# Attention with keys on the partitions, and a state scan made in four stretches

## What is computed

```python
def one_block(qblk):
    s = jnp.einsum('bgrqd,bgkd->bgrqk', qblk, kt).astype(jnp.float32) * scale
    p = jax.nn.softmax(s, axis=-1).astype(vt.dtype)
    return jnp.einsum('bgrqk,bgkd->bgrqd', p, vt)

def s5_bidirectional(u, ...):
    for direction, reverse in ((0, False), (1, True)):
        a_bar = jnp.exp(a * dt)                       # one complex number a state
        bu = jnp.einsum('blgp,gnp->blgn', ug, b_bar)
        _, states = lax.associative_scan(_linear_combine, (a_seq, bu), axis=1, reverse=reverse)
        y = y + jnp.einsum('blgn,gpn->blgp', states, c).real
```

## Time and profile before

| | us |
|---|---|
| median of 3 runs | 2836.97 |
| lowest, highest | 2826.1, 2838.0 |
| profiled execution, own time | 2827.34 |
| span of its trace | 2825.2 |
| the stage `heads` with its barriers, 547 to 904 | 357 |
| the stage `s5_outputs`, 904 to 1040 | 136 |

### The profile page before, as it was taken

One profiled execution on the slowest core, in us unless ns is written; L12 is line 12 of the kernel. 1 busy time (PEld: TensorE's weight loads), 2 busy tenths in 40 slices (PEclk: granted clock), 3 DMA queues, 4 the chain that ended last, 5 costly groups with the idle time before them and its releaser, 6 DMA issues. The chain is left out here.

```text
span 2825.2 us, 41292 instructions
## 1 busy us (share of the span) xinstructions
PE 2560.4 (91%) x15638; PEld 2207.0 (78%) x15638; DVE 1403.6 (50%) x2285; ACT 923.0 (33%) x1916; POOL 1134.5 (40%) x1244
## 2 busy tenths in 40 slices
PE   6999997699997868799799999999999699999798
PEld 6988886699996657677678888877777589998587
DVE  6464444687887936322654453555555522222314
ACT  4232222633333233223322223356565400000321
POOL 3454441177775125402054544433333355552320
PEclk9999999999998889899999999999999799999899
DMA  7323333201011464444343333343432464442543
GB/s 162 113 65 106 102 106 89 56 24 47 31 39 31 74 128 153 133 158 144 115 103 129 117 144 125 132 164 125 148 121 104 175 202 136 136 136 83 195 148 149
DMA packets 268360, 328.33 MB, mean 116 GB/s; under 512 B 45300, under 2 KB 216974, under 8 KB 267030
## 3 DMA queue, kind: packets, MB, share of 16 engines
q1 hardware_dynamic: 230006, 239.09, 28.3%
q10 hardware_dynamic: 38176, 86.78, 8.3%
HBM read 212.75 MB, written 103.55 MB: 112 GB/s over the span
## 5 line engine op out<-in xcount | busy, mean ns | idle before, releaser
L1025 POOL TENSOR_TENSOR w_hi<-w_raw,ones 128x512 fp32r<-128x512 f32 (+1 forms) x232 | 274.8, 1184 | 765.4 <-PE r L1036 263.8
L1027 POOL TENSOR_TENSOR w_lo<-w_raw,w_hi 128x512 fp32r<-128x512 f32 (+1 forms) x232 | 344.8, 1486 | 18.2
L1036 PE MATMUL r<-h_lo,w_hi 128*128 128x264 f32 (+1 forms) x864 | 286.6, 332 | 0.0
L1036 PE MATMUL r<-h_hi,w_lo 128*128 128x264 f32 (+1 forms) x864 | 278.5, 322 | 0.0
L1036 PE MATMUL r<-h_hi,w_hi 128*128 128x264 f32 (+1 forms) x864 | 277.6, 321 | 0.0
L1036 PE MATMUL r<-xc_lo,w_hi 128*128 128x264 f32 (+1 forms) x768 | 248.5, 324 | 28.4 <-POOL w_lo L1027 28.4
L1036 PE MATMUL r<-xc_hi,w_lo 128*128 128x264 f32 (+1 forms) x768 | 248.9, 324 | 0.0
L1036 PE MATMUL r<-xc_hi,w_hi 128*128 128x264 f32 (+1 forms) x768 | 248.4, 323 | 0.0
L434 POOL TENSOR_TENSOR w_lo<-w_raw,w_hi 128x512 fp32r<-128x512 f32 x64 | 85.2, 1359 | 251.0 <-ACT w_hi L500 251.0
L1036 PEld LDWEIGHTS r<-xc_lo,w_hi 128*128 128x128 f32 x768 | 146.0, 190 | 41.0 <-issue 28.9
L1036 PEld LDWEIGHTS r<-h_hi,w_hi 128*128 128x128 f32 x864 | 163.0, 189 | 16.2 <-issue 2.4
(11 more groups left out here) (345 smaller groups left out, 6376.0 us busy)
## 6 DMA issues: line engine op xcount, KB each, us to landing
w_raw<-in_w_in_even SPq DMA_DIRECT2D x72, 256.0 KB, 3.0
w_raw<-in_w_in_odd SPq DMA_DIRECT2D x64, 256.0 KB, 3.4
w_raw<-in_w_ogate SPq DMA_DIRECT2D x64, 256.0 KB, 7.1
v_d<-vs ACTq DMA_DIRECT2D x8, 1152.0 KB, 4.2
us<-u_d SPq DMA_DIRECT2D x128, 65.0 KB, 2.9
xc_d<-xc ACTq DMA_DIRECT2D x8, 1040.0 KB, 6.4
qk_d<-qk ACTq DMA_DIRECT2D x16, 520.0 KB, 2.7
sz_d<-sz SPq DMA_DIRECT2D x8, 1040.0 KB, 5.2
```

The source lines that it names most:

```text
L1025: self.nc.gpsimd.tensor_tensor(hi, raw, one, ALU.mult).then_inc(self.hi_done, 1)
L1027: self.nc.gpsimd.tensor_tensor(lo, raw, hi.bitcast(F32), ALU.subtract).then_inc(self.split, 1)
L1036: ins = self.nc.tensor.matmul(bank[:, 0:n], w[:, u % self.buffers, k, :], z[:, off:off + n], start=(first and k == 0 and w is self.hi and ...
```

## The change

**Attention.** The keys now lie on the partitions. A head's queries are two parts of 580 and 460 (`PARTS`), so there are 16 passes; in each, the nine blocks of 116 keys (`KEYS`) are steps. In a step PE makes the scores [116 keys, 580 or 460 queries] (`scores`), ACT copies them from the PSUM into the tile `prob` (`keep`), and DVE raises a running maximum `top` with them (`higher`: both inputs in SBUF). At the end of a pass PE turns `top` around (`turn_top`), DVE finds each query's maximum (`find`), PE spreads it over the partitions (`spread`), DVE subtracts it from the stored scores (`lower`: one input in SBUF, one in PSUM), ACT takes the exponential in place (`power`), and the result is already what PE needs as weights for the product with the values (`mix`), which come with a column of ones that gives the sum of each row. The 648 transposes of probabilities fall away; there are 72 for the maxima, 72 for spreading and 72 to turn the finished [queries, 128] tiles (`turn_rows`). A finished tile is copied by ACT, its sum inverted by DVE (`invert`), scaled by ACT, turned by PE and multiplied with the gate by DVE (`out`). The order of all this is written out by hand again: pass n's scores, pass n-1's subtraction and pass n-2's product with the values run in the same nine steps.

**Scan.** The 130 chunks, with two of zeros behind them, are four stretches of 33. POOL first scans the four side by side (32 steps: one product of 1024 columns and two additions of 512), then carries the ends of the stretches on (two steps with `far`, the 33rd power of `step`), and then adds to each chunk of the last three stretches what comes from the stretch before (32 steps: one product of 768 columns, two additions of 384). Every instruction waits for the one before it. It is written out, without a loop. `far` is made in `front` by 36 small DVE instructions and four copies. POOL's scratch is `pw_in`, which is not needed any more then; `s5_outputs` uses the same room.

The diff, cut to its core; the removed lines of `heads` and `s5_scan` are in the listing above.

```diff
-QT = [(0, 120), (120, 120), (240, 112), (352, 120), (472, 112), (584, 112),
-      (696, 120), (816, 112), (928, 112)]
+KEYS = [(i * 116, min(116, L - i * 116)) for i in range(NT)]
+PARTS = [(0, 580, 5, 116), (580, 460, 4, 115)]
+START = (222, 0)
...
-            vt = se.sb("v", [P, NT, KV * HD])
+            vt = se.sb("v", [P, NT, KV, HD + 1])
...
-            t["Z"] = se.sb("Z", [P, CH + 1, 2, G])
+            t["Z"] = se.sb("Z", [P, 1 + SUPER * LONG, 2, G])
...
+SUPER, LONG = 4, 33
 def s5_scan(nc, gp, t, tmp, steps, turns):
     do = Steps(gp, steps)
     tt = nc.gpsimd.tensor_tensor
+    z = t["Z"][:, 1:1 + SUPER * LONG, :, :].rearrange("p (s j) q g -> p s j (q g)", s=SUPER)
+    carry = tmp[1]
+    def product(now, factor):
+        n = now.shape[1]
+        out = tmp[0][:, 0:n * 4 * G].rearrange("p (s o q) -> p s o q", s=n, o=2)
+        do(tt(out, now.unsqueeze(2).broadcast_to([P, n, 2, 2 * G]),
+              t[factor][:, :, :].rearrange("p (o q) g -> p o (q g)", o=2).unsqueeze(1).broadcast_to([P, n, 2, 2 * G]),
+              ALU.mult))
+        return out[:, :, :, 0:G], out[:, :, :, G:2 * G]
+    def add(out, x, y):
+        do(tt(out, x, y, ALU.add))
+    def halves(x):
+        return x.rearrange("p s (o g) -> p s o g", o=2)
+    for j in range(1, LONG):
+        own, other = product(z[:, :, j - 1, :], "step")
+        now = halves(z[:, :, j, :])
+        add(now, now, own)
+        add(now, now, other)
+    for s in range(1, SUPER - 1):
+        own, other = product(z[:, s - 1:s, LONG - 1, :], "far")
+        now = halves(z[:, s:s + 1, LONG - 1, :])
+        add(now, now, own)
+        add(now, now, other)
+    left = z[:, 0:SUPER - 1, LONG - 1, :]
+    for j in range(LONG - 1):
+        own, other = product(left, "step")
+        add(carry[:, :, :, :], own, other)
+        left = carry[:, :, :, :].rearrange("p s o g -> p s (o g)")
+        now = halves(z[:, 1:SUPER, j, :])
+        add(now, now, carry[:, :, :, :])
...
-        tmp = s.sb("tmp", [P, 2, GB // 2, T, GP])
+        tmp = t["pw_in"][:, :, :, :].rearrange("p e q g -> p (e q g)").rearrange(
...
+                one, power = (pw[:, T, 0, :], pw[:, T, 1, :]), (X(0), X(1))
+                times(power, one, one)
+                for n in range((LONG - 1).bit_length() - 2):
+                    times(power, power, power)
+                times(power, power, one)
+                do.free(v.tensor_copy(t["far"][:, 0, :], X(0)))
...
+    LOWERED = {0: ((2, 8),), 3: ((1, 0),), 4: ((1, 1), (1, 2)), 5: ((1, 3),), 6: ((1, 4), (1, 5)), 7: ((1, 6),),
+               8: ((1, 7),)}
...
+        sb = s.sb("prob", [P, NB, NT, WIDE])
+        top, peak = s.sb("top", [P, WIDE]), s.sb("peak", [P, 5])
...
+                def scores(n, j):
+                    off, width, tiles, m = PARTS[n % 2]
+                    ko, kn = KEYS[j]
+                    g = n // 2 % KV
+                    if j == 0:
+                        pe.wait_ge(q_done, n + 1)
+                        if n >= 2:
+                            pe.wait_ge(found, n - 1)
+                        if n and turned_in[n - 1]:
+                            pe.wait_ge(yd, turned_in[n - 1])
+                    elif j == 1:
+                        if n >= 2:
+                            pe.wait_ge(low, NT * (n - 1))
+                    else:
+                        pe.wait_ge(kept, NT * n + j - 1)
+                    out = region(n, j)
+                    for o, w in HALVES[n % 2]:
                         for x, z in ((0, 1), (0, 0), (1, 0)):
+                            last = nc.tensor.matmul(out[0:kn, START[n % 2] + o:START[n % 2] + o + w],
+                                                    kr[z][:, g, ko:ko + kn], q[x][:, off + o:off + o + w],
+                                                    start=(z == 1), stop=(x == 1))
+                    last.then_inc(sc, 1)
...
+                def turn_top(n):
+                    off, width, tiles, m = PARTS[n % 2]
+                    pe.wait_ge(kept, NT * n + 8)
...
+                def mix(n, j):
+                    off, width, tiles, m = PARTS[n % 2]
+                    g = n // 2 % KV
+                    for x in range(j * tiles, (j + 1) * tiles):
+                        i, k = divmod(x, NT)
+                        w = DONE[n] + i
+                        if i == 0:
+                            pe.wait_ge(ex, NT * n + k + 1)
+                        if k == 0 and w >= 2:
+                            pe.wait_ge(taken, w - 1)
+                        kn = KEYS[k][1]
+                        last = nc.tensor.matmul(o_slot(w)[0:m, :], sb[0:kn, n % NB, k, i * m:(i + 1) * m],
+                                                vt[0:kn, k, g, :], start=(k == 0), stop=(k == NT - 1))
+                        if k == NT - 1:
+                            last.then_inc(pv, 1)
...
+                for n in range(LAST + 1):
+                    for j in range(NT):
+                        if n < NU:
+                            scores(n, j)
+                        if j == 2 and 1 <= n <= NU:
+                            spread(n - 1)
+                        if 2 <= n < LAST:
+                            mix(n - 2, j)
+                        for w in turned_at.get(n * NT + j, ()):
+                            turn_rows(w, n)
+                        if j == 0 and 1 <= n <= NU:
+                            turn_top(n - 1)
...
+                def keep(n, j):
+                    kn, width = KEYS[j][1], PARTS[n % 2][1]
+                    if j == 0 and n >= NB:
+                        act.wait_ge(pv, DONE[n - NB + 1])
+                    act.wait_ge(sc, NT * n + j + 1)
+                    nc.scalar.activation(sb[0:kn, n % NB, j, 0:width],
+                                         region(n, j)[0:kn, START[n % 2]:START[n % 2] + width],
+                                         ACT.Copy).then_inc(kept, 1)
+                def power(n, j):
+                    kn, width = KEYS[j][1], PARTS[n % 2][1]
+                    act.wait_ge(low, NT * n + j + 1)
+                    nc.scalar.activation(sb[0:kn, n % NB, j, 0:width], sb[0:kn, n % NB, j, 0:width], ACT.Exp,
+                                         scale=SCALE).then_inc(ex, 1)
...
+                for n in range(LAST + 1):
+                    for j in range(NT):
+                        for w in mixed_at.get(n * NT + j - 1, ()):
+                            take_rows(w)
+                        if n < NU:
+                            keep(n, j)
+                        for back, k in LOWERED.get(j, ()):
+                            if 0 <= n - back < NU:
+                                power(n - back, k)
+                        for w in mixed_at.get(n * NT + j - 1, ()):
+                            scale_rows(w)
+                        if j == 4 and n + 1 < NU:
+                            leading(n + 1)
...
+                def higher(n, j):
+                    kn, width = KEYS[j][1], PARTS[n % 2][1]
+                    dve.wait_ge(kept, NT * n + j + 1)
+                    now = sb[0:kn, n % NB, j, 0:width]
+                    if j == 1:
+                        if n:
+                            dve.wait_ge(tt, n)
+                        v.tensor_tensor(top[0:kn, 0:width], sb[0:kn, n % NB, 0, 0:width], now,
+                                        ALU.max).then_inc(raised, 1)
+                    else:
+                        dve.wait_ge(raised, (NT - 1) * n + j - 1)
+                        v.tensor_tensor(top[0:kn, 0:width], top[0:kn, 0:width], now, ALU.max).then_inc(raised, 1)
...
+                def lower(n, j):
+                    kn, width = KEYS[j][1], PARTS[n % 2][1]
+                    if j == 0:
+                        dve.wait_ge(sp_done, n + 1)
+                    dve.wait_ge(kept, NT * n + j + 1)
+                    x = sb[0:kn, n % NB, j, 0:width]
+                    at = SPREAD_AT[n % 2]
+                    v.tensor_tensor(x, x, region(n, NT + 1)[0:kn, at:at + width], ALU.subtract).then_inc(low, 1)
...
+                for n in range(LAST + 1):
+                    for j in range(NT):
+                        if j == 1 and 1 <= n <= NU:
+                            find(n - 1)
+                        for w in mixed_at.get(n * NT + j - 1, ()):
+                            invert(w)
+                        for w in out_at.get(n * NT + j, ()):
+                            out(w, n)
+                        for back, k in LOWERED.get(j, ()):
+                            if 0 <= n - back < NU:
+                                lower(n - back, k)
+                        if n < NU and j:
+                            higher(n, j)
+                        if j == 5 and n + 1 < NU:
+                            rest(n + 1)
```

More of the change, by code:

```diff
@@ new lines, in spread @@
+                def spread(n):
+                    off, width, tiles, m = PARTS[n % 2]
+                    pe.wait_ge(found, n + 1)
+                    pe.wait_ge(kept, NT * (n + 1))
+                    out = region(n, NT + 1)
```

(26 more changed lines are left out.)

296 lines of the change are left out of this document (133 added, 163 removed).

## The result

The changed kernel takes **2866.5 us** (median of 4 runs, 2865.5 to 2867.9) beside 2834.6 us for the kernel before (4 runs, 2826.1 to 2838.0): ratio **1.0117, 95% interval 1.0093 to 1.0142**. It is slower by 32 us. The forecast was 2833, and the likeliest case was no change, with a range of its own of 2819 to 2851; the measured time lies outside that, and at the upper edge of the wide range (2793 to 2868). Times near 2873 stood in the text as the third case, at 0.19.

What follows compares the result with a forecast made beforehand. PE was taken to bound attention now, with POOL's scan 8 us ahead; after the change, scan and attention would end near 898 and 893, saving 4 us: 2837 - 4 = 2833 us on the median's footing, range 2793 to 2868.

Steps and rivals of the forecast that it cites:

- the likeliest case: In `heads`, POOL's scan slowed by `higher` sets the end, attention close; stage within 14 us of now; chance 0.43.
- The third case: In attention, DVE becomes the bound, each `higher` waiting 0.97 us; stage 36 us later, whole 2873 us; chance 0.19.
- What a wait costs: In attention, DVE's `higher` and `rest` wait for POOL 0.65 us on average, 144 times, 94 us in all.
- `lower` pays nothing: In attention, DVE's `lower` reads PSUM and is free of sharing with POOL, staying near 0.76 us.
- POOL: The new scan takes 303 us alone, ending at 850; sharing with DVE adds 48 us, so it ends at 898.
- PE: In attention, PE's work falls from 342 to 301 us; were PE the bound, attention would end at 865.
- The step that failed: In attention, waits raise DVE from 243 to 337 us, passing PE's 301; attention ends near 893.
- DVE's own sum: DVE's instructions in attention take 30.4 us a head, 243 us in all, less than PE's 301.
- The skill's rule: DVE instructions with two SBUF inputs contend with POOL reading SBUF; the second blocks fully, for the whole instruction.
- 100 us of it for POOL: In the scan, POOL loses each `higher`'s whole length, 100 us; stage 47 us later, 2884 us; chance 0.06.
- the 48 that came from the rows of `ogate`: In the scan, each `higher` costs POOL 0.40 us at 580 columns, 0.27 at 460: 48 us.
- The 40 small instructions in `front`: On DVE in `front`, 8 to 10 us, hidden ahead of an 18.00 us idle gap, so nothing behind it moves.

Runs made afterwards that it cites:

- Experiment 1: The changed kernel with the state scan on POOL left out beside attention: 2785.9 us, ratio 0.9838 to the kernel before.
- experiment 12: The changed kernel without its scan, DVE filling 335 columns with zeros before each of 144 `higher` and `rest`: 2812.6 us, ratio 0.9932.
- Experiment 3: The kernel before with only the new scan, its attention as before: 2863.8 us, ratio 1.0114.
- experiment 2: The changed kernel with the running maximum reading the new scores from PSUM, PE waiting before it overwrites them: 2801.8 us, ratio 0.9892.
- the doses: Two runs of the changed kernel without its scan, DVE zero fills before 144 instructions: 745 columns, 2857.9 us; 335 columns, 2812.6 us.
- experiment 7: The changed kernel with the running maximum read from PSUM and the state scan left out: 2793.9 us, ratio 0.9867.
- experiment 4: The changed kernel with the scan of the kernel before: 2837.8 us, ratio 1.002.
- Experiment 5: The changed kernel with each product of the new scan made in two instructions of half the width: 2843.7 us, ratio 1.0036.
- experiment 9: The changed kernel with a finished row turned by PE one step later: 2863.3 us, ratio 1.0112.
- experiment 11: The changed kernel without its scan, DVE filling 745 columns with zeros before each of 144 `higher` and `rest`: 2857.9 us, ratio 1.0093.

## Why the prediction was wrong

Step by step, by its own numbers.

- **What a wait costs: right in all, with some luck.** 0.65 us on average for each of 144, 94 us in all, was the forecast; 0.68 and 98 were measured, and `higher` at 1.58 us for the "near 1.4" that was named. Beside the wide steps (to 741) a wait is 0.86 us where 0.75 was worked out, beside the adding steps 0.55 for 0.54, and the last 8 of the 144 come when POOL is done and wait for nothing, which the forecast had not taken off. It was also right that `lower` pays nothing.
- **POOL: right.** The scan was to end at 898, and at 850 if alone. It ends at 894.8; with the PSUM read, where POOL shares with 16 instructions only, at 851.5.
- **PE: nearly right.** 301 us were forecast, and attention's end at 865 with PE alone. Experiment 1 has 281 us, and 857.9: 20 us less work, and 13 us more idle time than the 17 that the forecast allowed up to attention's end, so the near hit is in part two errors against each other. The 302 us of the kernel after look like a hit and are none: they are experiment 1's 281 and 21 more for the same 2160 records at a lower clock (0.93 for 0.98).
- **The step that failed: what DVE's waits were added to.** The prediction added 94 us to DVE's own 243, got an end of 893, and compared it with PE's 865 and POOL's 898, as if three queues ran side by side and the longest decided. By that, DVE had 58 us of slack to give. DVE's own sum was not the fault: without POOL the window shows it busy 216 us, with the overlap of neighbours counted once, and the forecast's 243 is the sum of lengths. But the order of a pass closes a loop. PE's scores go to ACT's copy, DVE's maximum, PE's turn and spread, DVE's subtraction, ACT's exponential and back to PE, in a hand-written order with each engine's queue in it. A sum that fits the runs starts from PE's path and adds most of the waits to it: attention alone ends at 858, the waits add 98, and with shares of 0.66 to 0.86 that gives 923 to 942; 935.5 was measured (a share of 0.79). The share comes from the experiments and was not to be had from the profile before; with a share of 1 the same working would have said 956.
- **The third case** named this ("a late `higher` holds `turn_top`, ACT and then PE") and gave 2873, close to what came. That its time came out near is partly luck: it still compared the sums of queues, with a mean wait of 0.97 us that was not met, and held that it decides only from 0.80 on (its own sum passes POOL's 898 at 0.69). Attention set the end at 0.68, and in experiment 12 an addition of 0.23 us a piece (33 us over 144) already moves the end of attention by 23 us.
- **The skill's rule.** `higher`, with two inputs in SBUF, waits beside POOL, and `lower` does not. The Trainium skill, "SBUF — State Buffer", section Who interferes with whom, states just this of one and of two SBUF inputs; the trace agrees. For two SBUF inputs the full blocking that the prediction quotes stands in another section of that page, Summary: rules for kernel authors: the second to issue blocks until the first has finished. The prediction made 100 us of it for POOL; POOL lost 43, near the 48 that came from the rows of `ogate`, where 0.14 us of each start overlap. Experiment 3 met another sentence of Who interferes with whom, that a `tensor_scalar` can contend as well: the scaling takes 0.76 us at its shortest, 0.86 on average beside the old scan's short instructions and 1.60 beside the wide ones. The prediction had left that out.
- The 40 small instructions in `front` cost nothing that shows at the start of `heads`, 547 in both kernels. But 36 of them take 13.0 us, where 8 to 10 were forecast for all 40; the idle gap ahead of the copy of C shrinks from 18.00 to 3.49 us, and that copy starts 0.8 us later.

Where does the gain of the lighter PE go? Against the kernel before, attention without a scan gained 43 us (the old attention was not run without its scan, so this is the new one alone against the old one with it), and lost 78 to the scan that runs beside it. Of these 78, by the windows of experiment 1 and the kernel after, 57 are idle time of PE (86.6 us for 29.5) and 21 are PE's own work taking longer; by the ratio of the clocks, 0.98 to 0.93, some 15 of the 21 are the clock (an estimate). With experiment 2 most of it comes back, and that the cure is one operand of one instruction is the plainest sign that DVE's waits beside POOL are the cause.

What stays open: why the share is 0.7 in one case and 0.86 in another; by which of the waits in the loop DVE's lost time reaches PE, since the doses show only that it arrives, and the loop itself is read from the code and from one place of the timeline; and the 4 us that the kernel after loses behind the stage.

## What to carry to other kernels

When a step runs round a loop of three engines, don't just compare their sums: here 0.66 to 0.86 of the time that DVE lost was added to the stage, although DVE was idle nearly a third of the time. That it holds for the other engines of the loop was not tried. Wide GpSimd instructions are quick for GpSimd and dear for a DVE that needs two SBUF operands beside them; give DVE one operand from PSUM where it is still there, and cost the change for both engines. To test such a reading, put the suspected time back as a plain delay, at half size too: the half dose tells a sum from a maximum.

## What the runs showed of the hardware

- A DVE instruction that reads PSUM and SBUF takes the same time beside a busy POOL as without: 746 to 760 ns at 580 columns in experiment 2, 749 to 760 in experiment 7. With both inputs in SBUF it took 762 ns on average without POOL and 1580 with wide POOL instructions, but 851 beside the old scan of 128 columns an instruction (experiment 4; that scan also leaves POOL idle a quarter of the time). Experiment 5, with POOL as busy as before and its products half as long, has 1406. So the wait depends on how long the other engine's instruction is.
- A `tensor_scalar` over 1040 columns waited as well: 0.76 us at its shortest, 0.86 on average beside short POOL instructions and 1.60 beside wide ones.
- A gap of 3 us in PE's work was followed by 5.5 us at half clock (the windows above). Over the stage the granted clock was 0.98 with 30 us of PE's idle time (experiment 1) and 0.93 with 87 (the kernel after), but the sum of idle time alone does not give it: experiment 9 had 0.91 with 78, experiment 11 0.95 with 83.
- POOL's product of 1024 columns with a broadcast operand took 2.40 us on average in experiment 2, and 1.81 to 1.83 at 768 where undisturbed (the shortest and the median of the row below, L801 there). Both lie near the line through the earlier trace rows (2.41 and 1.85): the product with a broadcast operand costs what the line through plain ones gives.

```profile
L801 POOL TENSOR_TENSOR pw_in<-scan,step x31: 1812/1829/2227, 723.1 to 847.5; 128x768 f32<-128x768 f32 x31
```
